# A two-layer decoder trunk on one core: a new table of weight slots, one modulation block moved to GpSimd, and more value groups between the output projections

## The chip, the core and the metric

The kernel runs on one core of a Trainium2 chip. TensorE (PE) multiplies and transposes, VectorE (DVE) does the elementwise work and the selections, ScalarE (ACT) copies out of PSUM and applies functions, GpSimd (POOL) computes a little and issues the gathers, and SyncE (SP) issues the weight loads. All transfers run on 16 DMA engines. The metric is the device time of one execution in microseconds; lower is better.

## What is computed

Two layers over 256 tokens of width 1024, all in float32, weights read from HBM. Cut from the reference:

```python
for l in range(DEPTH):                                   # DEPTH = 2
    mod = (silu(c) @ w_ada[l] + b_ada[l])                # six blocks of 1024
    sh1, sc1, g1, sh2, sc2, g2 = split(mod, 6)
    h = rms_norm(x) * (1.0 + sc1) + sh1
    q, k, v, qi, ki, wi, cu = split(h @ w_in[l], offs)
    attn = dsa_attention(q, k, v, qi, ki, wi)            # top-64 keys, causal
    conv = conformer_conv(cu, ...)                       # GLU, 31 causal taps, norm, silu
    mixed = concat([rms_norm(attn, ..), rms_norm(conv, ..)])
    x = x + g1 * (mixed @ w_out[l])
    h2 = rms_norm(x) * (1.0 + sc2) + sh2
    x = x + g2 * peer_ffn(h2, peer_wq[l], sub_keys[l], u[l], v[l])
```

`peer_ffn` picks 128 experts for every token (8 heads, 16 each). It gathers a row of `u` for each (4 KB), takes its dot product with `h2`, and sums the gathered rows of `v` with the resulting coefficients.

## The kernel before

**Parts.** A part `p` (0 to 3) is one layer `l = p // 2` with 128 tokens `t = p % 2`. For every part GpSimd issues 128 gathers of u rows and 128 of v rows, each 0.5 MB (128 tokens by 4 KB). They land in a ring of 13 row buffers, the tile `rows`. DVE takes one dot product per u row (L1512, function `dots_to`); PE sums four v rows in a group (L893, function `v_to`, 32 groups a part). While the rows of part p pass, PE, ACT and DVE compute projections, attention and expert choice of part p+1. Between GpSimd's gathers and their consumers there is only the ring: a buffer is used again when its dot (`u_used`) or its group (`v_used`) is done.

**Weights.** SP loads all weights in pieces of 1 MB, in the one order that `plan()` writes out. Every piece has a slot, and SP waits for the last user of the slot's former piece (`wait_weight_used`, loop at L609) before it issues the next. Nothing behind a waiting load is issued. Later on there are four slots (`wring`). In part 0, before the first gather, seven more exist. Slots 4 to 6 and 7, 8 lie in rows 6 to 11 and rows 0 to 3 of the row ring, slots 9 and 10 in `spread_c`. Rows 4 and 5 hold the convolution's accumulator `acc` and its temporaries `tap_tmp`. GpSimd's first gathers wait until the slot that shares their row buffer was used for the last time (`wait_slot_free`), and they are issued in order from row 0.

**Modulation blocks.** `mod` has twelve blocks of 4 MB each (four pieces). For most, PE multiplies the block (L760, 16 matmuls, job "ada") and turns the result later ("adaT"). DVE sums two of them, (0,2) and (0,4), with `ada_product`. The table `ADA` says where in each part a block is taken. Block (1,1), the scale of layer 2, is a PE product at place (0,"S"), in the middle of part 0's attention.

**Part 0, the path to the first gather.** DVE does 93 convolution tap steps for three of four channel groups, in pieces between its other work (`taps`, L1494). GpSimd does the fourth group by a TENSOR_SCALAR (L650) and a TENSOR_TENSOR (L651) for each tap. Then PE turns `acc`, DVE normalises (`conv_norm`, `join`, L1711), PE turns the mixed rows and projects them (L774), DVE adds to x and normalises, and PE projects the first expert queries (`wq` block 0, L802). DVE chooses 16 experts of head 0 and writes `u_at` (L1784), and the gathers begin. The blocks `wq` 1 to 3 (L788) follow on PE, with block (1,3) of the modulation between the second and the third.

**Later parts.** In `second(p)` PE mixes groups of the running v sum into the attention and the projections of the next part, by the table `V_GROUPS`. Then comes `mT` (two turns of the mixed rows), a wait for ACT's copy of them, and the four pieces of the output projection (L820), with a group behind the first three. On DVE, `qk_norms` (L1607 to L1612) runs without a break between runs of dots.

## Time and profile before

| | us |
|---|---|
| median of 3 runs | 1762.42 (1762.26 to 1763.1) |
| the profiled execution, device time | 1759.5 |
| its span, first to last instruction | 1757.2 |
| PE / DVE / POOL / ACT busy | 1020.7 / 1104.3 / 1021.9 / 262.9 |
| bytes moved | 693.84 MB at a mean of 395 GB/s |

A busy share near 60% on three engines says that none of them is full for long. The views to read are those of the DMA: its rate in each stretch of the span, and beside it which engine GpSimd's and SP's issues wait for. The table of 40 slices on the page shows a rate of 409 GB/s in the slices without a gap, and 249 GB/s in the lowest, around 150 us.

### The profile page before, as it was taken

Reading aid. Unit: us, or ns where it says so; the run is one execution under the profiler, and the core shown is the slowest. Engines: PE = TensorE matmul, PEld = TensorE weight load, DVE = VectorE, ACT = ScalarE, POOL = GpSimd, SP = SyncE. Lnnn points to the kernel's source line nnn. Section 1 sums busy time; section 2 is a strip of 40 time slices with the busy share of each in tenths; the row PEclk is TensorE's granted clock in tenths of the full one; section 3 lists DMA queues with packets and bytes.
Section 4 is the critical chain, followed back from the end, with each engine's and each line's share of the span. In section 5 each row is a group of like instructions: output and inputs, shape, how many; then the busy total and the mean of one; then the engine's idle time right before and its main releaser. Section 6 shows DMA issues by size and latency. Waiting matters only on the chain.

```text
span 1757.2 us, 17710 instructions
## 1 busy us (share of the span) xinstructions
PE 1020.7 (58%) x5918; PEld 566.7 (32%) x5918; DVE 1104.3 (63%) x3003; ACT 262.9 (15%) x710; POOL 1021.9 (58%) x1132
## 2 busy tenths in 40 slices
PE   5988796513887579611798568810679620004554
PEld 2646673311354156400246145600226300001111
DVE  1987997798218586889315766789622979991000
ACT  1131232301110024400100022600210100000000
POOL 2620535467654764566655674467655777776774
PEclk9978898556998779855799779965789965557888
DMA  9996999999999999999999999999999999999998
GB/s 351 389 346 249 405 402 409 409 380 409 393 409 401 409 409 395 396 410 410 406 368 408 409 406 404 409 409 409 404 385 408 400 411 410 409 410 404 409 409 325
DMA packets 199404, 693.84 MB, mean 395 GB/s; under 512 B 23943, under 2 KB 23959, under 8 KB 199315
## 3 DMA queue, kind: packets, MB, share of 16 engines
q0 software_dynamic: 147776, 537.19, 77.3%
...
HBM read 691.60 MB, written 1.05 MB: 394 GB/s over the span
## 4 chain that ended last, share of the span: by engine, by line
DMA 38%; PE 24%; DVE 15%; POOL 14%; issue 7%; ACT 1%; SPq 0%; POOLq 0%; DVEq 0%; ACTq 0%
DMA rows<-in_peer_v,v_at 18%; DMA rows<-in_peer_u,u_at 17%; PE ps L893 8%; DVE rows L1512 7%; POOL rows L667 7%; POOL rows L675 7%; PE ps L848 6%; DMA wring<-in_w_in 2%; PE ps L820 2%; DVE rows L1494 2%; PE ps L788 1%; DMA rows<-in_w_ada 1%; PE ps L836 1%; PE ps L706 1%; PE ps L774 1%
## 5 line engine op out<-in xcount | busy, mean ns | idle before, releaser
L667 POOL DMA_INDIRECT rows<-in_peer_u,u_at x512 | 482.8, 943 | 386.0 <-DVE dots L1512 213.1
L1512 DVE CUSTOM_DVE_ANT_0 rows<-rows,ps 128x1024 f32<-128x1024 f32 x512 | 609.8, 1219 | 101.5 <-DMA rows<-in_peer_u,u_at 88.7
L675 POOL DMA_INDIRECT rows<-in_peer_v,v_at x512 | 488.6, 954 | 281.4 <-PE ps L893 148.7
L893 PE MATMUL ps<-rows,spread_c 128*32 128x512 f32 x2048 | 324.8, 764 | 196.0 <-DMA rows<-in_peer_v,v_at 195.9
L706 PE MATMUL ps<-ident,coef 128*128 128x128 f32 x4 | 1.9, 475 | 349.7 <-DVE coef L1848 349.7
L893 PEld LDWEIGHTS ps<-rows,spread_c 128*32 128x32 f32 x2048 | 70.4, 126 | 399.1 <-issue 396.7
L848 PEld LDWEIGHTS ps<-hT,wring 128*128 128x128 f32 x1184 | 141.0, 200 | 25.3 <-issue 23.3
L848 PE MATMUL ps<-hT,wring 128*128 128x128 f32 x1184 | 146.3, 286 | 1.2 <-ACTq L1188 1.2
L820 PE MATMUL ps<-wring,hT 128*128 128x512 f32 x256 | 123.4, 627 | 13.3 <-DMA wring<-in_w_in 7.0
L1216 ACT ACTIVATE diag_eq<-ident,cwT 128x128 f32<-128x128 f32 x372 | 111.2, 387 | 31.6 <-PE ps L874 30.3
L706 PEld LDWEIGHTS ps<-ident,coef 128*128 128x128 f32 x4 | 0.7, 182 | 352.4 <-DVE coef L1848 352.4
L874 PE MATMUL ps<-diag_eq,hc 128*128 128x128 f32 x744 | 101.9, 301 | 19.9 <-ACT diag_eq L1216 19.9
L1525 DVE TENSOR_TENSOR gy<-ps,g 128x512 f32<-128x512 f32 x8 | 5.5, 690 | 163.2 <-PE ps L893 163.1
L874 PEld LDWEIGHTS ps<-diag_eq,hc 128*128 128x128 f32 x744 | 97.2, 213 | 27.1 <-ACT diag_eq L1216 25.3
L1716 DVE MAX8 v<-mixed_use 128x8 f32<-128x128 f32 x64 | 15.6, 285 | 121.0 <-ACTq L1176 119.1
L1173 ACT COPY mixed_use<-ps 128x512 f32<-128x512 f32 (+1 forms) x54 | 30.7, 569 | 300.9 <-PE ps L848 142.4
L820 PEld LDWEIGHTS ps<-wring,hT 128*128 128x128 f32 x256 | 48.4, 199 | 76.2 <-issue 57.3
L1815 DVE TENSOR_TENSOR gy<-ps,g 128x512 f32<-128x512 f32 x8 | 5.5, 692 | 81.2 <-PE ps L820 78.5
L1421 ACT ACTIVATE dots<-dots 128x128 f32<-128x128 f32 x4 | 1.2, 309 | 361.6 <-DVE dots L1512 361.6
L760 PE MATMUL ps<-wring,cact 128*32 128x512 f32 x208 | 32.1, 744 | 23.4 <-DMA wring<-in_w_ada 23.4
L1512 DVE DVE_READ_ACCUMULATOR2_ANT dots<- 128x1 f32 x512 | 42.2, 82 | 0.0
L1184 ACT ACTIVATE hT<-ps,modcol 128x128 f32<-128x128 f32 x52 | 19.5, 456 | 141.4 <-PE ps L706 140.6
...
## 6 DMA issues: line engine op xcount, KB each, us to landing
...
rows<-in_peer_u,u_at POOLq DMA_INDIRECT x512, 14.4
rows<-in_peer_v,v_at POOLq DMA_INDIRECT x512, 9.0
...
```

What stands on the lines that cost most here:

```text
L667: pool.indirect_dma_start(row(n), None, u_rows, bass.IndirectOffsetOnAxis(ap=u_at[:, p % 2, k:k + 1], axis=0)).then_inc(row_landed[n % SLO ...
L675: pool.indirect_dma_start(row(n), None, v_rows, bass.IndirectOffsetOnAxis(ap=v_at[:, p % 2, tok:tok + 1], axis=0)).then_inc(row_landed[n % ...
L706: ins = pe.transpose(o[:, i * n:(i + 1) * n], s, ident[0:n, 0:n])
L760: ins = pe.matmul(o[32 * g:32 * g + 32, :], cact[:, k:k + 1].to_broadcast([P, 32]), ws[:, i, 512 * cc:512 * cc + 512], start=h == 0, stop= ...
L820: ins = pe.matmul(o, lhs[:, k, :], w[:, j, 512 * cc:512 * cc + 512], start=k == 0, stop=k == KT - 1)
L848: ins = pe.matmul(o[:, i * P:(i + 1) * P], w[:, j, at:at + P], rhs[:, k, :], start=False, stop=(k, i) == (KT - 1, 3))
L874: ins = pe.matmul(o[:, cols], hc[:, ct, t * P + i:t * P + i + P], tap_diag(p, n, i - i0), start=False, stop=i == TAPS - 1)
L893: ins = pe.matmul(ps[32 * g:32 * g + 32, YB + q, :], spread_c[:, g, a, :], row(n)[:, q * 512:q * 512 + 512], start=a == 0, stop=a == 31)
L1173: act.copy(dst, o if src is None else src(o)).then_inc(free[b], 1)
L1216: ins = act.activation(tap_diag(p, n, i - i0), ident[:, :], ACT.Copy, scale=cwT[:, ct, i:i + 1])
L1494: seq_.lag(stt(o, hc[:, ct, i:i + P], w, o, ALU.mult, ALU.add))
L1512: dve.tensor_tensor_reduce(out=row(n), in0=row(n), in1=h2_shown, scale=1.0, scalar=0.0, op0=ALU.mult, op1=ALU.add, accum_out=dots[:, k:k + ...
```

## The change

- **A twelfth slot.** Rows 4 and 5 become slot 9 (`LATE_SLOT`), free once the convolution was turned (`conv_full`); the two slots in `spread_c` are now 10 and 11. The slots of part 0 from `sk` on come from a table (`SLOTS_OF`). All eight pieces of `wq` 0 to 3 have slots that don't wait for a `wq` before them, and the pieces of block (1,3) come behind them. The blocks that share row buffers 0 to 3 and 4 to 7 with gathers are now `wq` 1 and `wq` 2.
- **Block (1,1) goes to GpSimd.** It is neither in SP's order nor a PE product. GpSimd, behind its taps, loads it in four pieces through slots 7 and 8, and sums it with 8 TENSOR_SCALAR and 7 TENSOR_TENSOR of 128x1024 into half of `diag_eq`. SP waits for the end of that (`pool_ada_taken`) before it loads `wq` 1 into the same slots. PE turns the sum behind `wq` 3.
- **Block (1,3)** is multiplied behind `wq` 3, not between `wq` 1 and `wq` 2, and turned in the tail.
- **V groups.** One group of v rows is added between `mT` and the output projection in every part from 1 on; in parts 1 and 3 one more stands before the attention. Later groups move up by one.
- **Norms split.** `qk_norms` of parts 1 to 3 does 8 dots between the reciprocal roots and the multiplications. In part 1 the run of dots before it has 18, not 24.

```diff
-FIRST_WSLOTS = 11
+FIRST_WSLOTS = 12
+LATE_SLOT = 9
-V_GROUPS = [((4, 7), 8, (9, 10, 11), 12), ((4, 5, 6, 7), 9, (10, 11, 12), 13)]
+V_GROUPS = [(3, (4, 7), 8, 9, (10, 11, 12), 13), (4, (5, 6, 7, 8), 9, 10, (11, 12, 13), 14)]
+POOL_ADA = (1, 1)
+POOL_SLOTS = (7, 8)
-    (0, "S"): [product(1, 1), turn(1, 0), turn(1, 1)],
+    (0, "S"): [turn(1, 0)],
-    (0, "wq1"): [product(1, 3)],
-    (0, "wq2"): [turn(1, 3)],
-    (0, "tail"): [product(0, 5), product(1, 4), turn(0, 5), turn(1, 4)],
+    (0, "wq"): [turn(1, 1), product(1, 3)],
+    (0, "tail"): [turn(1, 3), product(0, 5), product(1, 4), turn(0, 5), turn(1, 4)],
+SLOTS_OF = {("sk", 0): (2,), ("ada", 0, 3): (3, 4, 5, 6), ("out", 0, 0): (0, 1), ("adav", 0, 4): (LATE_SLOT, 2, 3, 4),
+            ("out", 0, 1): (5, 6), ("wq", 0, 0): (0, 1), ("wq", 0, 1): POOL_SLOTS, ("wq", 0, 2): (LATE_SLOT, 4),
+            ("wq", 0, 3): (2, 3), ("ada", 1, 3): (0, 1, 2, 3)}
@@ SyncE
+                if name == ("wq", 0, 1):
+                    sp.wait_ge(pool_ada_taken, 4)
                 if use_before[i] is not None:
                     wait_weight_used(sp, use_before[i])
+                elif slot == LATE_SLOT:
+                    sp.wait_ge(conv_full, 1)
@@ GpSimd, behind the taps
+            for h in range(2):
+                wait_weight_used(pool, max(i for i, u in enumerate(uses) if slot_of[i] == POOL_SLOTS[h] and i < n_pool))
+                load_ada(h)
+            for h in range(4):
+                w = weight_slot(POOL_SLOTS[h % 2]).rearrange("p (k n) -> p k n", k=2)
+                pool.wait_ge(pool_ada_landed[h % 2], 16 * (h // 2 + 1))
+                for i in range(2):
+                    k = 2 * h + i
+                    dst = ada_sum if k == 0 else w[:, i, :]
+                    seq_(pool.tensor_scalar(dst, w[:, i, :], cact[:, k:k + 1], None, ALU.mult))
+                    if k:
+                        seq_(pool.tensor_tensor(ada_sum, ada_sum, w[:, i, :], ALU.add), pool_ada_taken if i else None)
+                if h < 2:
+                    load_ada(h + 2)
@@ TensorE, second(p)
                     v_to(p - 1, 2)
                     logits(p, CHUNKS[t][1])
-                    v_to(p - 1, 3)
-                    attend(p, at[0])
-                    v_to(p - 1, at[1])
+                    v_to(p - 1, at[0])
+                    attend(p, at[1])
+                    v_to(p - 1, at[2])
                 ... mT ...
+                v_to(p - 1, at[3])
                 pe.wait_ge(mixedT_ready, 2 * (p + 1))
@@ VectorE, qk_norms(p, between)
+                if between:
+                    between()
                 seq_(tt(qk, qk, rs[:, 0:16].unsqueeze(2).to_broadcast([P, 16, DH]), ALU.mult))
```

GpSimd's queue, from its last tap to its first gathers. Before:

```order
L650 TENSOR_SCALAR rows<-hc,cwT 128x128
L651 TENSOR_TENSOR rows<-rows 128x128
L667 DMA rows<-in_peer_u,u_at 128x1024 x96
L664 MEMSET spread_c 128x4096
L667 DMA rows<-in_peer_u,u_at 128x1024 x32
```

And now, up to the third of the block's four pieces:

```order
L666 TENSOR_SCALAR rows<-hc,cwT 128x128
L667 TENSOR_TENSOR rows<-rows 128x128
L674 DMA rows<-in_w_ada 128x2x1024 x2
L687 TENSOR_SCALAR diag_eq<-rows,cact 128x1024
L687 TENSOR_SCALAR rows<-rows,cact 128x1024
L689 TENSOR_TENSOR diag_eq<-diag_eq,rows 128x1024
L674 DMA rows<-in_w_ada 128x2x1024
L687 TENSOR_SCALAR rows<-rows,cact 128x1024
L689 TENSOR_TENSOR diag_eq<-diag_eq,rows 128x1024
L687 TENSOR_SCALAR rows<-rows,cact 128x1024
L689 TENSOR_TENSOR diag_eq<-diag_eq,rows 128x1024
L674 DMA rows<-in_w_ada 128x2x1024
```

Four loads and fifteen operations of 1024 columns now stand between the taps and the first gather.

SP's queue around `wq` (its weights are `in_peer_wq`), with what each load waits for. Before:

```order
L609 DMA rows<-in_peer_wq 128x4x512 [waits bank1_full]
L609 DMA rows<-in_peer_wq 128x4x512 [waits piece_used]
L609 DMA wring<-in_peer_wq 128x4x512 [waits ada_taken] x2
L609 DMA wring<-in_w_ada 128x2x1024 [waits ada_taken] x2
L609 DMA rows<-in_w_ada 128x2x1024 [waits piece_used]
L609 DMA rows<-in_w_ada 128x2x1024 [waits bank1_full]
L609 DMA wring<-in_peer_wq 128x4x512 [waits piece_used]
L609 DMA wring<-in_peer_wq 128x4x512 [waits bank2_full]
L609 DMA wring<-in_peer_wq 128x4x512 [waits piece_used] x2
```

And now, from the load that waits for the convolution:

```order
L625 DMA rows<-in_w_ada 128x2x1024 [waits conv_full]
L625 DMA wring<-in_w_ada 128x2x1024 [waits bank0_full]
L625 DMA wring<-in_w_ada 128x2x1024 [waits piece_used]
L625 DMA rows<-in_w_ada 128x2x1024 [waits piece_used]
L625 DMA rows<-in_w_out 128x4x512 [waits piece_used]
L625 DMA rows<-in_w_out 128x4x512 [waits bank3_full]
L625 DMA wring<-in_peer_wq 128x4x512 [waits piece_used]
L625 DMA wring<-in_peer_wq 128x4x512 [waits bank2_full]
L625 DMA rows<-in_peer_wq 128x4x512 [waits bank1_full,pool_ada_taken]
L625 DMA rows<-in_peer_wq 128x4x512 [waits piece_used,pool_ada_taken]
L625 DMA rows<-in_peer_wq 128x4x512 [waits ada_taken] x2
L625 DMA wring<-in_peer_wq 128x4x512 [waits ada_taken] x2
```

The last four pieces of `wq` wait for DVE's sum of block (0,4), where they waited for PE to be through with `wq` 1 and with block (1,3). One load waits for the convolution, and the next `wq` for GpSimd.

PE's queue in part 1, from the last values of the attention to the second piece of the output projection. Before, with L893 the groups of v rows:

```order
L918 MATMUL ps<-vals,mixed_use 128x64 x4
L893 MATMUL ps<-rows,spread_c 32x512 x16
L706 MATMUL ps<-ident,hb 128x128 x8
L820 MATMUL ps<-wring,hT 128x512 x4
L893 MATMUL ps<-rows,spread_c 32x512 x8
```

And now, with L935 the same groups:

```order
L960 MATMUL ps<-vals,mixed_use 128x64 x4
L935 MATMUL ps<-rows,spread_c 32x512 x8
L746 MATMUL ps<-ident,hb 128x128 x8
L935 MATMUL ps<-rows,spread_c 32x512 x8
L862 MATMUL ps<-wring,hT 128x512 x4
L935 MATMUL ps<-rows,spread_c 32x512 x8
```

One group stands between the turns of the mixed rows and the first piece of the projection.

## Rows read from the trace of the kernel before

**Rows 1.** The page: rates in 40 slices, and bytes of all transfers.
```profile
GB/s 351 389 346 249 405 402 409 409 380 409 393 409 401 409 409 395 396 410 410 406 368 408 409 406 404 409 409 409 404 385 408 400 411 410 409 410 404 409 409 325
DMA packets 199404, 693.84 MB, mean 395 GB/s; under 512 B 23943, under 2 KB 23959, under 8 KB 199315
```
**Rows 2.** Stretches: busy PE, PEld, DVE, ACT, POOL, then PEclk, DMA share, GB/s.
```profile
120.00:180.00 60.00, 52.27 (x304) 34.81 (x302) 42.01 (x148) 10.95 (x24) 4.89 (x5) 0.90 0.69 256
160.00:170.00 10.00, 10.00 (x92) 10.00 (x91) 6.42 (x38) 1.49 (x4) 0.00 (x0) 1.00 0.01 2
...
370.00:380.00 10.00, 1.11 (x4) 0.71 (x4) 9.86 (x19) 0.58 (x1) 5.54 (x6) 0.50 0.97 347
440.00:450.00 10.00, 10.00 (x83) 5.48 (x86) 6.01 (x16) 4.25 (x12) 7.56 (x9) 1.00 0.94 334
860.00:900.00 40.00, 32.65 (x144) 11.58 (x144) 10.65 (x33) 2.28 (x8) 23.03 (x24) 0.87 0.95 360
1280.00:1300.00 20.00, 17.90 (x73) 6.48 (x66) 0.00 (x0) 2.28 (x8) 10.60 (x12) 0.87 0.94 355
```
**Rows 3.** SP's timeline: start, length, merged loads.
```profile
105.19 21.55 SPq L609 DMA_DIRECT2D wring<-in_w_ada  x4
141.86 3.80 SPq L609 DMA_DIRECT2D rows<-in_w_ada  x2
171.80 5.02 SPq L609 DMA_DIRECT2D wring<-in_peer_wq  x4
```
**Rows 4.** DVE's timeline to the first experts: last taps, second norm of join, u_at.
```profile
105.57 6.13 DVE L1494 SCALAR_TENSOR_TENSOR rows<-hc,cwT,rows 128x128 f32<-128x128 f32 x23
114.24 0.70 DVE L1698 BATCH_NORM_STATS2 bn<-ps 128x6 f32<-128x512 f32 x1 [1.30 <-PE ps L1053]
125.89 0.48 DVE L1711 TENSOR_SCALAR hb<-hb,rs 128x512 f32<-128x512 f32 x1
172.62 0.17 DVE L1784 CAST u_at<-expert 128x16 uint32<-128x16 f32 x1
```
**Rows 5.** PE's timeline: turns of mixed rows, wq 1, wq 2.
```profile
128.82 1.09 PE L706 MATMUL ps<-ident,hb 128*128 128x128 f32 x8
165.35 7.31 PE L788 MATMUL ps<-hT,wring 128*128 128x128 f32 x64
181.83 9.01 PE L788 MATMUL ps<-hT,wring 128*128 128x128 f32 x64 [3.73 <-issue]
```
**Rows 6.** Single operations by line: shortest, median and longest in ns, and when.
```profile
L1494 DVE SCALAR_TENSOR_TENSOR rows<-hc,cwT,rows x2: 339/466/593, 98.3 to 98.6; 128x128 f32<-128x128 f32 x2
L1494 DVE SCALAR_TENSOR_TENSOR rows<-hc,cwT,rows x11: 339/341/343, 99.1 to 101.8; 128x128 f32<-128x128 f32 x11
L651 POOL TENSOR_TENSOR rows<-rows x30: 452/455/1101, 58.2 to 98.6; 128x128 f32<-128x128 f32 x30
L650 POOL TENSOR_SCALAR rows<-hc,cwT x30: 602/708/1662, 57.2 to 97.8; 128x128 f32<-128x128 f32 x30
L626 POOL TENSOR_TENSOR halves<-ident x1: 195/195/195, 2.9 to 2.9; 128x2 f32<-128x2 f32 x1
L664 POOL MEMSET spread_c<- x1: 3530/3530/3530, 355.5 to 355.5; 128x4096 f32 x1
```
**Rows 7.** POOL's timeline: last tap, first gather, a norm, v gathers.
```profile
98.60 0.45 POOL L651 TENSOR_TENSOR rows<-rows 128x128 f32<-128x128 f32 x1
173.67 1.10 POOL L667 DMA_INDIRECT rows<-in_peer_u,u_at  x1 [74.62 <-DVE u_at L1784]
725.20 0.94 POOL L667 DMA_INDIRECT rows<-in_peer_u,u_at  x1 [8.19 <-DVE dots L1512]
881.89 0.94 POOL L675 DMA_INDIRECT rows<-in_peer_v,v_at  x1 [8.00 <-PE ps L893]
```
**Rows 8.** PE's timeline in part 2, at the turns and the first projection piece.
```profile
869.92 1.09 PE L706 MATMUL ps<-ident,hb 128*128 128x128 f32 x8 [0.89 <-DVE hb L1711]
873.11 6.67 PE L820 MATMUL ps<-wring,hT 128*128 128x512 f32 x8 [2.10 <-ACTq L1188]
```

67 lines of the change are left out of this document (40 added, 27 removed).

## The prediction

> **What bounds the kernel now.** Read the page's line of rates first. In most of the 40 slices the core moves 405 to 411 GB/s, whatever the engines do, so the DMA is the full resource; the bytes are 693.84 MB [rows 1]. I take 409.5 GB/s as the full rate. All bytes at that rate are 1694.4 us, and the span is 1757.2 us, so the DMA has lost 62.8 us. The change moves no byte more or less. Its time is the old one plus what it changes in these losses.
>
> Next, where they lie. Between 120 and 180 us the rate is 256, a loss of 60 x (1 - 256/409.5) = 22.5 us, and from 160 to 170 nothing moves at all [rows 2]. The smaller holes, by the same formula: 860 to 900, 4.8 us; 1280 to 1300, 2.7; 440 to 450, 1.8; 370 to 380, 1.5 [rows 2]. Start, tail and slices slightly under the full rate make up the rest, and the change doesn't touch them.
>
> The large hole has two sides. SP has issued 54 pieces by 145.7 us and then nothing until 171.8 [rows 3]: every slot is held. The gathers start at 173.67, since POOL waited 74.62 us for `u_at` [rows 7]. So the end of the hole is set by the compute path to the first 16 experts. On that path, from about 99 us on, DVE is never idle for long: taps from 105.57, turned convolution at 114.24, second norm of `join` at 125.89 to 126.37, `u_at` at 172.62 [rows 4]. PE turns the mixed rows only at 128.82 [rows 5], 2.4 us after DVE was ready, since it was at block (0,3).
>
> **Part 1: the slots, with an unchanged path.** A piece is 1.05 MB, 2.56 us at full rate. Before, 54 pieces are in by about 158, and the next bytes flow at 173.5. Now the same 54 can be in (50 of SP, 4 of POOL), and two of block (1,3) follow when `wq` 0 is done, near 164 us: 56 pieces, 5.1 us more work before the gathers. But the gathers pay it back. Rows 0 to 3 share slots with `wq` 1, which PE ends at 172.7 [rows 5], so four gathers go. Row 4 shares its slot with `wq` 2. That block starts now at once, at about 174.5, since its weights are there and no product stands before it, and takes 7.3 to 9.0 us [rows 5]. Its first piece is free near 181.6. Four gathers are 2.1 MB or 5.1 us of work, in by about 180.7; the next bytes flow at about 183.4. That costs 2.7 us. Two small gaps come in besides: SP now stands at its late slot until the convolution is turned (about 114), and six pieces issued near 91 plus POOL's two last to about 112.5. Counting pieces up to the point where the DMA is full for good, before has moved 57.7 pieces by 183.5, and now 58 by 183.4. The slots alone are worth 1 us, no more: a gain in the hole that the row buffers give back. PE loses its product of (1,1), but it waits for DVE's taps behind it anyway, so that is worth nothing.
>
> **Part 2: POOL's sum, and what it does to DVE.** This is the largest term. In the last tap of POOL, a TENSOR_TENSOR from 98.60 to 99.05 [rows 7], DVE's tap of 98.6 took 593 ns; the eleven taps after it, with POOL idle, took 341 [rows 6]. A DVE operation with two SBUF inputs stands still while POOL's two-input operation runs, for 0.25 us of its 0.452. In the other direction, POOL's shortest TENSOR_TENSOR is 452 ns and its longest 1101 [rows 6], beside a DVE operation of 1024 columns. POOL's TENSOR_TENSOR grows from 195 ns at 2 columns to 452 at 128 [rows 6], 2.04 ns a column; at 1024 it is 2.28 us, and holds DVE for about 2.28 - 0.2 = 2.1. There are seven: 14.7 us. POOL's TENSOR_SCALAR takes 602 ns at 128 columns [rows 6]. For 1024 the lower bound is 602 plus 896 columns at the memset's 0.86 ns (3530/4096, rows 6), 1.37 us, and the upper 8 x 602, 4.8 us. I take 1.4: the 195 ns row shows that most of a short operation is fixed cost. Next to it the DVE taps show no delay that I can see, at 128 columns.
>
> When does it happen? POOL's two first loads are issued at 99.5 and share the DMA with SP's, so they land near 107 and 112. A column block costs 1.4 + 2.3 + 0.2 us, so the eight and their loads run from 107 to about 138. In that stretch DVE is on the path. Laying seven holds of 2.1 us over DVE's own row of operations moves the end of `join` from 126.3 to about 138.5; 12.1 us arrive there, since two fall partly on waits. The 2.4 us that DVE was early go off. So the mixed rows are turned 9.7 us later, and with them `u_at`, the first gather and the end of the hole: **plus 9.7 us**, minus the 1 us of part 1. The DMA can't use that time: SP has no free slot. `pool_ada_taken` at 138 costs nothing: SP comes to that wait at 138.4 plus 9.7, and `wq` 1 is needed at 165.4 plus 9.7. At the upper price of TENSOR_SCALAR POOL ends near 161; `wq` 1 then lands by 169, still in time, and queued behind it are `wq` 2 and 3 only.
>
> The Trainium skill says more (SBUF — State Buffer, "Who interferes with whom"): the pair of ports is an exclusive lock for the whole instruction, and a DVE operation with two SBUF inputs contends with any GpSimd operation that reads SBUF. The rows on TENSOR_TENSOR agree. By that rule TENSOR_SCALAR of 1024 columns holds DVE too, which no row here shows; it is the slower rival below.
>
> **Part 3: v groups.** In part 2, PE ends the turns at 871.0 and idles 2.10 us for ACT's copy, then a projection piece takes 6.67 us, and POOL waits 8.00 us until 881.89 for a group [rows 7, 8]. A group is 1.92 us of PE work and fits into that idle time; its rows have landed, since groups arrive every 5.1 us and the last began at 865.4. POOL gets four buffers at about 872.9 and doesn't stop at all, and in-flight rows cover the 6.67 us. Of the 4.8 us I take 4.5. The hole at 1280 to 1300 is the same figure in part 3: 2.4 of 2.7. At 440 the group before the attention frees four buffers some 6 us sooner: 1.6 of 1.8. Sum 8.5 us. Low end 4, if PE has to wait for the added group's rows and brings the projection later; high end 9.3, all of it.
>
> **Part 4: split norms.** POOL stops 8.19 us at 717 to 725 for DVE's norms [rows 7], as it does in part 1 at 368. With 8 dots in the middle (8 x 1.28 us, the pace of the DMA) both stops are shorter than what is in flight. I count the 1.5 us of 370 to 380 [rows 2] less 0.3, and 0.9 for the smaller ones in parts 2 and 3: 2.0 us, between 0.5 and 3. Its price is that `qk_ready` comes 10 us later, hidden behind PE's wait for the coefficients.
>
> **Sum.** +9.7 - 1 - 8.5 - 2.0 = -1.8 us. From the profiled execution's 1759.5 that is 1757.7; the median lies 2.9 us above the profiled one, so 1762.42 - 1.8 = 1760.6.
>
> **Rivals.** (a) *The holds don't grow with the operation.* 128 columns can't tell a lock of a whole instruction from one of short chunks. If POOL lets DVE in between chunks, DVE loses perhaps 0.25 us for each of 7, or a third of the 14.7: the path moves 0 to 6 us. For it speaks that the taps beside TENSOR_SCALAR don't suffer; against it that DVE's blocked tap ended only when POOL's did. Time: 1762.4 - 1 - 10.5 + (0 to 6), 1751 to 1757. (b) *POOL's TENSOR_SCALAR holds DVE too*, for the 0.88 us in which 1024 columns stream at the memset's rate. Eight of them are 7 us, of which DVE gives way to about half between its own operations: the path moves by 13.3, not 9.7, and the v groups and norms can't outweigh it if they bring 8 or less. Sum 13.3 - 1 - 8 = +4.3: 1766.7, slower. It decides from a delay of `u_at` by more than 15 us on, or from 13 with a poor part 3. If TENSOR_SCALAR costs its upper 4.8 us and holds as well, the delay passes 20 and the time 1770. (c) *The groups bring little*, since PE waits for rows as it does with most groups now: part 3 is 4 and the sum +2.7: 1765. (d) *The GpSimd sum is hidden after all*, as its loads land later than I think and the holds fall on DVE's waits behind 126: that gives the times of (a).
>
> **How the numbers follow.** Forecast (delay 8 to 12 us): 0.40. Rival (a) and (d): 0.32. Rival (b): 0.18. Rival (c): 0.10. The forecast's own range is 1757 to 1765. A measurement of this kernel tells 0.2% or 3.5 us from no change. Faster by more than that: all of (a) and (d), and 0.08 of the forecast: 0.40. Slower: 0.14 of (b) and 0.05 of (c): 0.19. The rest, 0.41, is within. The range that leaves 2 in 10 out goes from 1752.5 to 1768.
>
> **What would show it.** In the trace after: the first gather near 183 us, not 173.7; DVE taps between 107 and 116 with single durations over 2 us, each ending with a TENSOR_TENSOR of POOL (2.3 us); POOL's TENSOR_SCALAR near 1.4 us; a second gap in the DMA after the fourth gather, 2 to 3 us long; 860 to 900 and 1280 to 1300 at 400 GB/s or more; POOL's waits of 8 us at 717 and 874 gone. If the first gather stays near 174, the forecast is too high by 9 us. If `wq` 1 keeps PE waiting for its weights, POOL's sum took longer than its upper price, and part 2 is wrong there.

## The result, and the profile after

The changed kernel takes 1770.84 us (median of 7 runs, 1769.77 to 1772.79). The kernel before, run beside it, takes 1762.42 us (median of 7, 1760.82 to 1766.78). The ratio is 1.0045, 95% interval 1.0034 to 1.0055: slower by 8 us. The forecast was 1760.6, and its range ended at 1768.0. The profiled execution took 1770.62 us, with a span of 1768.8.

The page again first, the rates in 40 slices and the bytes, as in [rows 1]:

```profile
GB/s 354 381 297 276 304 402 409 409 389 395 409 409 402 409 408 400 403 402 409 398 409 405 401 396 405 409 409 409 394 384 409 409 410 410 409 410 405 409 409 326
DMA packets 199403, 693.84 MB, mean 392 GB/s; under 512 B 23942, under 2 KB 23958, under 8 KB 199314
```

The bytes are the same and the full slices are as full as before. The third to fifth slice are worse together (297, 276, 304 for 346, 249, 405). The same stretches as in [rows 2], moved where the later start moves them (busy PE, PEld, DVE, ACT, POOL, then PEclk, DMA share, GB/s):

```profile
120.00:180.00 60.00, 46.77 (x216) 30.66 (x216) 47.70 (x87) 10.20 (x23) 36.45 (x15) 0.76 0.77 272
140.00:160.00 20.00, 19.63 (x59) 10.32 (x59) 19.46 (x13) 0.17 (x1) 17.58 (x6) 0.84 0.50 152
180.00:190.00 10.00, 9.28 (x83) 9.09 (x82) 8.97 (x49) 1.17 (x2) 2.06 (x3) 1.00 0.47 170
380.00:420.00 40.00, 7.81 (x24) 5.62 (x24) 39.55 (x71) 4.24 (x6) 26.61 (x29) 0.50 0.98 371
440.00:450.00 10.00, 6.60 (x41) 1.95 (x38) 8.27 (x24) 1.09 (x4) 7.57 (x9) 0.83 1.03 409
860.00:900.00 40.00, 32.03 (x176) 11.04 (x169) 5.99 (x23) 4.79 (x11) 29.54 (x33) 0.88 1.02 409
1300.00:1320.00 20.00, 20.00 (x90) 6.40 (x81) 0.00 (x0) 0.62 (x3) 11.81 (x13) 0.93 0.96 352
```

The hole before the first gather is now two holes, 140 to 160 and 180 to 190. The holes at 440 and at 860 to 900 are gone. Those at 380 to 420 (before 370 to 390) and at 1300 to 1320 (before 1280 to 1300) stay. With the formula of the prediction in stretches of 10 us, the losses up to 240 us are 47.4 us, before 33.8. From 240 to 1620 us, in stretches of 20, they are 18.0, before 19.8. So the whole increase lies ahead of 240 us.

There the first gather has moved by 13.7 us from the 173.67 of [rows 7]. GpSimd's timeline in the changed kernel, for its sum and the first gathers:

```profile
109.95 5.32 POOL L687 TENSOR_SCALAR diag_eq<-rows,cact 128x1024 f32<-128x1024 f32 x1 [8.20 <-DMA rows<-in_w_ada]
115.36 2.84 POOL L687 TENSOR_SCALAR rows<-rows,cact 128x1024 f32<-128x1024 f32 x1
118.29 2.37 POOL L689 TENSOR_TENSOR diag_eq<-diag_eq,rows 128x1024 f32<-128x1024 f32 x1
...
155.23 2.79 POOL L689 TENSOR_TENSOR diag_eq<-diag_eq,rows 128x1024 f32<-128x1024 f32 x1
187.33 1.08 POOL L707 DMA_INDIRECT rows<-in_peer_u,u_at  x1 [29.31 <-DVE u_at L1828]
...
194.73 1.11 POOL L707 DMA_INDIRECT rows<-in_peer_u,u_at  x1 [2.58 <-PE ps L830]
```

A TENSOR_SCALAR of 1024 columns takes 2.84 us undisturbed, not 1.4; the first took 5.32, beside DVE's taps. A TENSOR_TENSOR takes 2.37 to 2.79. The sum therefore ends at 158.0 us, not at 138. The fifth gather waits 2.58 us for `wq` 2: that is the second gap of part 1, forecast at 2.7.

DVE's timeline in the same kernel, for the taps beside the first TENSOR_SCALAR, operations of the convolution's norm and of the second norm of `join`, two steps of DVE's own sum of block (0,4), and the operation that reads PE's second output block:

```profile
106.43 6.13 DVE L1536 SCALAR_TENSOR_TENSOR rows<-hc,cwT,rows 128x128 f32<-128x128 f32 x23
...
119.28 1.92 DVE L1746 TENSOR_TENSOR hb<-hb,ln_gb 128x512 f32<-128x512 f32 x1
121.24 2.19 DVE L1747 TENSOR_TENSOR hb<-hb,ln_gb 128x512 f32<-128x512 f32 x1
...
125.35 2.00 DVE L1480 SCALAR_TENSOR_TENSOR newt<-rs,halfv 128x1 f32<-128x1 f32 x1
...
129.24 1.32 DVE L1755 TENSOR_SCALAR hb<-hb,rs 128x512 f32<-128x512 f32 x1
130.59 2.71 DVE L1492 CUSTOM_DVE_ANT_0 gy<-hb 128x512 f32<-128x512 f32 x1
...
142.52 3.25 DVE L1524 SCALAR_TENSOR_TENSOR rows<-wring,cact,rows 128x1024 f32<-128x1024 f32 x1
145.80 2.02 DVE L1525 SCALAR_TENSOR_TENSOR rows<-wring,cact,rows 128x1024 f32<-128x1024 f32 x1
...
158.60 0.69 DVE L1859 TENSOR_TENSOR gy<-ps,g 128x512 f32<-128x512 f32 x1
```

The 23 taps take 6.13 us, exactly as in [rows 4], although GpSimd's TENSOR_SCALAR runs beside the last 2.6 of them. The forecast had single taps of over 2 us there; there are none. After 118.29, when the first TENSOR_TENSOR begins, operations take 1.92 and 2.19 us instead of 0.69, a step of one column 2.00 instead of 0.22, and the root's sum of squares 2.71 instead of 0.69. Not all of these lie beside a TENSOR_TENSOR: the 2.19 us at 121.24 begin after the first one has ended (120.66), while GpSimd issues a load (120.95 to 121.71) and starts its next TENSOR_SCALAR (121.76). In the sum of (0,4) steps take 3.25 and 2.02 us instead of 1.28. PE's timeline shows what this passes on:

```profile
137.05 1.97 PE L746 MATMUL ps<-ident,hb 128*128 128x128 f32 x8 [7.10 <-DVE hb L1755]
140.37 9.79 PE L816 MATMUL ps<-wring,hT 128*128 128x512 f32 x16 [1.35 <-DVEq L1852]
149.99 7.03 PE L816 MATMUL ps<-rows,hT 128*128 128x512 f32 x16
...
179.01 7.31 PE L830 MATMUL ps<-hT,rows 128*128 128x128 f32 x64
```

The mixed rows are turned at 137.05, 8.2 us later than in [rows 5], after an idle time of 7.10 us. The first block of the output projection then takes 9.79 us; in the kernel before, the same 16 matmuls are the first half of the 14.00 us that the two blocks take together. The granted clock is 0.60 from 130 to 140 and 0.71 from 140 to 150. The second block ends at 157.02, and DVE reads it at 158.60 without having waited for it; in the kernel before, DVE waited 2.62 us for that block. So the path runs through DVE's sum here and not through PE's slower block. `wq` 1 begins at 179.01, against 165.35.

The result and the first set of runs (`e1_no_sum` to `e4_slots_pe`) fell on times at which the kernel before took 1762 to 1764 us. The later sets, those of every label that ends in `_only` but `e2_scale_only`, in `_mended`, `_again` or `_third`, fell on times at which the kernel before itself took 1946 to 1949 us. Its trace then has waits of PE, ACT and DVE under "issue" and "remote" in all parts (of ACT up to 54.8 us at a time), where the first trace has none of ACT and DVE and none of PE over 5.5 us; that the engines waited for their own instructions is my reading of these names and is not shown. The ratios of these sets are compared with one another and not with those of the first set.

### The profile page after: what moved, and what is told of

It reads as the page before. It is cut to its first block, busy times and chain, and to the rows that moved or that the text cites. A ratio compares the mean times of both kernels' runs of the same rounds, so it can differ in the third digit from the quotient of the medians.

```text
span 1768.8 us, 17681 instructions
## 1 busy us (share of the span) xinstructions
PE 1023.6 (58%) x5894; PEld 569.9 (32%) x5894; DVE 1120.9 (63%) x3003; ACT 263.0 (15%) x709; POOL 1071.1 (61%) x1151
## 4 chain that ended last, share of the span: by engine, by line
DMA 40%; DVE 21%; PE 19%; POOL 13%; issue 6%; ACT 1%; SPq 0%; DVEq 0%; POOLq 0%; ACTq 0%
DMA rows<-in_peer_v,v_at 19%; DMA rows<-in_peer_u,u_at 17%; DVE rows L1554 9%; PE ps L935 7%; POOL rows L715 7%; PE ps L890 6%; POOL rows L707 6%; DMA wring<-in_w_in 2%; DMA rows<-in_w_ada 1%; PE ps L862 1%; PE ps L878 1%; DVE rows L1536 1%; PE ps L816 1%; DVE newt L1480 1%; PE ps L746 1%
## 5 line engine op out<-in xcount | busy, mean ns | idle before, releaser
L935 PE MATMUL ps<-rows,spread_c 128*32 128x512 f32 x2048 | 329.1, 773 | 206.1 <-DMA rows<-in_peer_v,v_at 206.0
L935 PEld LDWEIGHTS ps<-rows,spread_c 128*32 128x32 f32 x2048 | 71.3, 127 | 405.4 <-issue 403.1
L862 PE MATMUL ps<-wring,hT 128*128 128x512 f32 x256 | 117.1, 600 | 8.2 <-DMA wring<-in_w_in 7.7
L746 PE MATMUL ps<-ident,hb 128*128 128x128 f32 x88 | 19.4, 394 | 37.0 <-DVE hb L1616 16.3
```

Source lines behind the costliest of these rows:

```text
L746: ins = pe.transpose(o[:, i * n:(i + 1) * n], s, ident[0:n, 0:n])
L862: ins = pe.matmul(o, lhs[:, k, :], w[:, j, 512 * cc:512 * cc + 512], start=k == 0, stop=k == KT - 1)
L935: ins = pe.matmul(ps[32 * g:32 * g + 32, YB + q, :], spread_c[:, g, a, :], row(n)[:, q * 512:q * 512 + 512], start=a == 0, stop=a == 31)
```

## Experiments

**Which part of GpSimd's block moves the path?** Three kernels take the changed one and leave out operations of the sum; the loads, the slots and all waits stay.

```diff
@@ e1_no_sum: no arithmetic
-                    seq_(pool.tensor_scalar(dst, w[:, i, :], cact[:, k:k + 1], None, ALU.mult))
-                    if k:
-                        seq_(pool.tensor_tensor(ada_sum, ada_sum, w[:, i, :], ALU.add), ...)
+                    if k == 0:
+                        seq_(pool.memset(ada_sum, 0.0))
@@ e2_scale_only: the 8 TENSOR_SCALAR stay
-                    if k:
-                        seq_(pool.tensor_tensor(ada_sum, ada_sum, w[:, i, :], ALU.add), ...)
@@ e6_add_only: the 7 TENSOR_TENSOR stay
-                    seq_(pool.tensor_scalar(dst, w[:, i, :], cact[:, k:k + 1], None, ALU.mult))
```

> The kernel after, with GpSimd's loads of block (1,1) kept and its 15 operations of 1024 columns left out (a MEMSET of zeros stands for the sum, so the scale of layer 2 lacks this block). Theory H: GpSimd's TENSOR_TENSOR holds DVE, and that alone moves the path to u_at. Then DVE's join ends near 127 us again, the mixed rows are turned near 129, out(0,0) takes about 7 us and not 9.8, the first gather stands within 2 us of 173.7 (after: 187.3), and the time is 1770.8 - 13.7 = about 1757, 1756 to 1760. Rival S (the new slots, the wait of SP at its late slot, the sharing of the DMA with GpSimd's loads): the first gather stays later than 180 and the time above 1765.

Measured: 1758.94 us beside 1763.53 of the kernel before, ratio 0.9977 (0.9963 to 0.9991). The first gather, the turns of the mixed rows and the first output block of this kernel, from GpSimd's and PE's timelines:

```profile
172.60 1.06 POOL L707 DMA_INDIRECT rows<-in_peer_u,u_at  x1 [58.97 <-DVE u_at L1828]
...
128.37 1.10 PE L746 MATMUL ps<-ident,hb 128*128 128x128 f32 x8
130.81 7.13 PE L816 MATMUL ps<-wring,hT 128*128 128x512 f32 x16 [1.35 <-DVEq L1852]
```

All three are back where they were, and the output block takes 7.13 us. Against the ratio 1.0045 of the full change the arithmetic costs 0.0068 of 1763 us, 12.0 us. The rival that blamed slots, SP's wait at the late slot, or the sharing of the DMA falls: all of these are in this kernel. What it doesn't have is SP's late release by `pool_ada_taken`; the kernel with the additions alone, below, ends its sum at 133 us and still has the late first gather, so that wait isn't what moves the path.

> The kernel after with GpSimd's 8 TENSOR_SCALAR of 1024 columns kept and its 7 TENSOR_TENSOR left out (the products are made, their sum is not). Theory H (only the TENSOR_TENSOR holds DVE): the first gather is within 1.5 us of that of the kernel without any arithmetic, so 174 to 176, and the time within 2 us of that kernel's. Rival L (a lock by any GpSimd instruction with an SBUF input, as my rival b had it): the first gather is 4 to 7 us later than without arithmetic, 179 to 182, and the time 4 to 7 us above. DVE's operations beside a TENSOR_SCALAR: no single one over 1 us by H, several at 2 us or more by L.

Measured: 1759.28 us, ratio 0.9981 (0.9967 to 0.9995), 0.3 us above the kernel without arithmetic. By time alone, theory H holds. The traces say otherwise of its reason. Three operations of DVE in the norms, and GpSimd's last TENSOR_SCALARs, in the kernel with scaling alone:

```profile
119.33 1.69 DVE L1745 TENSOR_TENSOR hb<-hb,ln_gb 128x512 f32<-128x512 f32 x1
...
126.04 1.85 DVE L1491 CUSTOM_DVE_ANT_0 gy<-hb 128x512 f32<-128x512 f32 x1
...
129.28 1.01 DVE L1483 SCALAR_TENSOR_TENSOR rs<-newt,rs 128x1 f32<-128x1 f32 x1
...
119.34 5.79 POOL L687 TENSOR_SCALAR rows<-rows,cact 128x1024 f32<-128x1024 f32 x2
...
126.22 11.91 POOL L687 TENSOR_SCALAR rows<-rows,cact 128x1024 f32<-128x1024 f32 x4
```

DVE's TENSOR_TENSOR takes 1.69 us, 1.00 more than its usual 0.69, and it began with GpSimd's TENSOR_SCALAR at 119.34. The two others are 1.16 and 0.85 us over theirs; they too begin within 0.2 us of a TENSOR_SCALAR. So a TENSOR_SCALAR does hold DVE's operations with two SBUF inputs, for about 1 us at its start and not for its 2.9; what DVE does in the rest of it takes its usual time in this trace. In the changed kernel one row doesn't fit: DVE's TENSOR_SCALAR at 129.24 takes 1.32 us instead of 0.49, though GpSimd's TENSOR_SCALAR had begun at 127.44, and ends (130.56) just after that one does (130.29). Why that happens there and not here (the same line takes 0.49 us at 130.33) is open. The last operation of `join` begins 14.5 us after the convolution's statistics here (115.80 to 130.33), and 11.7 without arithmetic. But PE, which came to the mixed rows 2.4 us late in any case, swallows nearly all of these 2.9 us. My expectation had "no single one over 1 us" for H: that is wrong, and rival L is right about the mechanism and wrong about the time.

> The kernel after with GpSimd's 7 TENSOR_TENSOR kept and its 8 TENSOR_SCALAR left out (a MEMSET starts the sum; the block isn't scaled by silu(c)). Times from the first statistics of the convolution to the first gather: after 71.6 us, scaling only 59.4, neither 58.7. If only TENSOR_TENSOR holds DVE, all the 12.8 us stay: 71 to 72 and a time of 1770. If both hold, and the 2.4 us that DVE is early cover the first of it, it is 58.7 + (7 x 2.0, less what falls after the path or on waits, less 2.4), about 67 to 70, and the time 1766 to 1769.

The times of this kernel are from the later conditions (1915.39 us beside 1945.94, ratio 0.9846, 0.9803 to 0.9890) and say nothing on the path. Its trace up to the first gather does. DVE's last step of the taps, GpSimd's second and third TENSOR_TENSOR, and the first gather:

```profile
111.35 5.65 DVE L1539 SCALAR_TENSOR_TENSOR rows<-hc,cwT,rows 128x128 f32<-128x128 f32 x3
...
114.49 4.78 POOL L687 TENSOR_TENSOR diag_eq<-diag_eq,rows 128x1024 f32<-128x1024 f32 x2
...
184.07 1.06 POOL L707 DMA_INDIRECT rows<-in_peer_u,u_at  x1 [50.98 <-DVE u_at L1828]
```

Three taps of together 1.12 us take 5.65: they end with the first of these two TENSOR_TENSOR, and the one before (109.52 to 113.45) held them as well. From statistics to first gather it is 65.8 us, below the 67 to 70 expected, since here one of the holds falls before the statistics. The last tap of GpSimd is the better mark, since nothing of the change lies before it and executions differ by up to 3 us there (98.15 to 101.17 in these traces). From it to the first gather, in one execution of each:

| kernel | last tap | first gather | between |
|---|---|---|---|
| before | 98.60 | 173.67 | 75.1 |
| e1_no_sum | 98.23 | 172.60 | 74.4 |
| e2_scale_only | 99.51 | 175.20 | 75.7 |
| e6_add_only | 98.15 | 184.07 | 85.9 |
| after | 99.46 | 187.33 | 87.9 |
| e4_slots_pe | 101.17 | 178.19 | 77.0 |

Adding alone costs 11.5 us, scaling alone 1.3, both 13.5. On top of adding, scaling costs 2.0. The figure for adding is the weakest, since it comes from the later conditions: the twelve traces without the sum there spread from 74 to 78 us (`before_again` 74.8, `n_third` 78.0).

In this kernel DVE isn't held in its sum of (0,4), and there PE's slower block is on the path: it takes 8.85 us instead of 7.13, and DVE waits 4.34 us for the second block instead of 2.62.

**Is the rest of the change worth having?** Two kernels separate it from the sum. The first is the kernel before with the new v groups and split norms. The second keeps the whole change, but gives block (1,1) back to SP and PE, and SP's wait for GpSimd goes:

```diff
@@ e4_slots_pe, from the changed kernel
-    (0, "S"): [turn(1, 0)],
+    (0, "S"): [product(1, 1), turn(1, 0), turn(1, 1)],
-    (0, "wq"): [turn(1, 1), product(1, 3)],
+    (0, "wq"): [product(1, 3)],
+SLOTS_OF = {("ada", 1, 1): (7, 8, 0, 1), ("sk", 0): (2,), ("ada", 0, 3): (3, 4, 5, 6), ("out", 0, 0): (7, 8),
+            ("adav", 0, 4): (0, 1, LATE_SLOT, 2), ("out", 0, 1): (3, 4), ("wq", 0, 0): (5, 6), ("wq", 0, 1): (7, 8),
+            ("wq", 0, 3): (0, 1), ("wq", 0, 2): (LATE_SLOT, 4), ("ada", 1, 3): (2, 3, 0, 1)}
```

> The kernel before with only the changed v groups and the split norms. My prediction had 8.5 + 2.0 = 10.5 us for these two: 1752. From the trace of the kernel after (DMA losses from 240 us to 1620 us 17.3 against 20.1 before) it would be 2.8: 1759.6. The hole at 1280 to 1300 stays if it belongs to the groups themselves, and is gone if it came from the later start of everything in the kernel after.

> The kernel after with block (1,1) back on SP and PE: loaded behind (0,2)'s place as before, multiplied by PE in the middle of part 0's attention. Late slot, table of slots, wq behind one another, v groups and norms stay as in the kernel after. By theory H the first gather comes back to 174 to 176 and the time is 1762.4 - 2.8 - 1 = 1758 to 1760, so it is faster than both kernels. By rival S (slots and order of loads cost the time) the first gather is later than 180 and the time above 1765.

Measured: 1757.77 us, ratio 0.9966 (0.9954 to 0.9978), and 1757.87 us, ratio 0.9964 (0.9951 to 0.9977). Both beat both kernels. Groups and norms together bring 6.0 us (3.9 to 8.1), between the 10.5 of the prediction and the 2.8 that the trace of the changed kernel alone suggested. That trace misled me, since the profiled execution of the kernel before was itself 3 to 4 us better than its median; I had noted the 2.9 us in the prediction and then compared two traces without it. The kernel before scatters from 1757.1 to 1769.6 over 34 runs, this one from 1755.4 to 1760.0 over 12.

The slots bring nothing measurable: with them it is 0.9964, without 0.9966. The first gather of `e4_slots_pe` is at 178.19, later than the 174 to 176 expected. The gap behind the fourth gather is there as in the changed kernel. GpSimd's timeline, fifth gather:

```profile
185.58 1.10 POOL L680 DMA_INDIRECT rows<-in_peer_u,u_at  x1 [2.54 <-PE ps L801]
```

The path is also 2.6 us longer than in `e1_no_sum` (table). DVE is ready for the mixed rows at 128.89 and PE turns them at 132.69, while in `e1_no_sum` it is 125.99 and 128.37: PE, with a product more ahead of it, is 1.4 us of that later. Up to 240 us this kernel loses 38.1 us of DMA time, and `e3_groups_norms` 35.4 with its first gather 2.8 us sooner (175.36): the trace shows no gain from the slots to set against the later gather.

**Why do two holes stay?** In the kernel with groups and norms, the windows that held the holes, DVE's and GpSimd's timelines in the norms of part 1, and PE's timeline at the mixed rows of part 3:

```profile
1280.00:1300.00 20.00, 15.51 (x68) 5.67 (x68) 4.33 (x17) 2.28 (x8) 12.21 (x14) 0.83 0.96 360
360.00:400.00 40.00, 7.81 (x24) 5.61 (x24) 39.17 (x76) 4.23 (x6) 24.98 (x27) 0.50 0.98 368
860.00:900.00 40.00, 30.23 (x149) 10.50 (x144) 8.93 (x27) 2.28 (x8) 26.67 (x29) 0.95 1.03 409
...
358.98 1.81 DVE L1610 TENSOR_SCALAR halfv<-halfv 128x16 f32<-128x16 f32 x1
...
357.22 3.53 POOL L664 MEMSET spread_c<- 128x4096 f32 x1
...
1284.91 1.97 PE L706 MATMUL ps<-ident,hb 128*128 128x128 f32 x8 [4.50 <-DVE hb L1714]
```

The hole at 860 to 900 is full here (409, before 360). At 1280 to 1300 it is 360, before 355, and PE waits 4.50 us for DVE's mixed rows. My theory was that the group of v rows added ahead of the attention delays everything behind it. The other kernels of the first set have the same table of groups, and their traces can be laid beside it: from PE's turn of the coefficients to its turn of the mixed rows, in us, and the slowest stretches of 20 us between 420 and 1340, in GB/s.

| kernel | part 1 | part 2 | part 3 | slowest 20 us |
|---|---|---|---|---|
| before | 45.5 | 43.6 | 47.6 | 880 to 900, 340; 1280 to 1300, 355 |
| after | 46.9 | 43.3 | 50.5 | 1300 to 1320, 352 |
| e3_groups_norms | 45.7 | 43.6 | 50.5 | 1280 to 1300, 360; 1240 to 1260, 362 |
| e1_no_sum | 47.7 | 43.5 | 48.9 | 460 to 480, 377 |
| e2_scale_only | 45.9 | 45.9 | 48.6 | 880 to 900, 352 |
| e4_slots_pe | 46.5 | 45.3 | 48.6 | 880 to 900, 352 |

With one table the hole falls in part 3 in two kernels, in part 2 in two, and in part 1 in one. Each time PE has waited 4.5 to 5.0 us for DVE's mixed rows and turns them in 1.97 us instead of 1.09, at the lower clock (granted 0.68 from 1280 to 1290 in `e3_groups_norms`). Part 2 has no group added ahead of its attention. So the added group alone doesn't put the hole at 1280 to 1300: where there is no hole it makes part 3 about 1 us longer than before (48.6 to 48.9 beside 47.6), and where the rest falls is open. Nor is the hole at 860 to 900 gone for good: with the same groups it is 378 and 381 GB/s in `e2_scale_only` and `e4_slots_pe`.

In the norms, a TENSOR_SCALAR of 16 columns takes 1.81 us instead of 0.17, and ends at 360.79, when GpSimd's MEMSET of 3.53 us ends. The split starts the norms 6 dots sooner, and that is beside the MEMSET. The Trainium skill (SBUF — State Buffer, "Who interferes with whom") says that `tensor_scalar` is among DVE's operations that can enter a mode which takes the port pair shared with GpSimd, and that in this mode DVE contends with GpSimd; this row agrees. The same section calls the pair an exclusive lock, held for a whole instruction: of TENSOR_TENSOR the traces here agree (DVE's step of one column at 125.35 ends at 127.35, GpSimd's TENSOR_TENSOR at 127.34), of TENSOR_SCALAR beside DVE's operations with two SBUF inputs they don't (1.0 us of 2.9).

Kernels with the groups alone and with the norms alone, and one that takes the added group of part 3 away and moves the MEMSET, were then run:

```diff
@@ e5_mended and mended_*, from e3_groups_norms
-                at = V_GROUPS[t]
+                at = V_GROUPS[t] if p != 3 else (3, (4, 5, 6, 7), 9, 10, (11, 12, 13), 14)
-                    if (p, k) == (0, 96):
+                    if (p, k) == (0, 112):
```

`v_only`, `v_again` and `v_third` are the kernel before with the first of the two edits of the change (`V_GROUPS` and the `v_to` calls), `n_only`, `n_again` and `n_third` with the second (`qk_norms`). `e7_slots_pe_mended` and `e7_third` are `e4_slots_pe` with the two lines above.

> The kernel before with the changed v groups alone. With both, groups and norms, the time was 0.9966 of before, -6.0 us (-4 to -8). If my shares of 8.5 for the groups and 2.0 for the norms are right in proportion, the groups alone bring -4.8 us. From that kernel's trace I expect more of it here than that: the hole at 860 to 900 (4.8 us) and the one at 440 (1.7) are gone, the one at 1280 to 1300 (2.4) stays, since the group added before the attention of part 3 delays the mixed rows. So -6.5 plus what comes back elsewhere: 0.9965, 0.995 to 0.998.

> The kernel before with the split norms alone. My prediction had -2.0 us. From the trace of groups and norms together: in part 1 the losses at 360 to 400 are 4.1 us against 3.2 before, at 720 they are less by 1.4 and at 740 more by 1.0. So it brings nothing: 0.999 to 1.001. In part 1 DVE's TENSOR_SCALAR of 16 columns inside the norms (0.17 us) takes 1.8 us again, ending with GpSimd's MEMSET, if that MEMSET is what held it.

> Before with groups and norms, and two things mended. In part 3 the group added before the attention is taken away: groups 3, (4 to 7), 9, 10 stand where 4, (5 to 8), 9, 10 stood. And GpSimd's MEMSET of the spread matrix stands before gather 112 of part 0, not before gather 96. If the hole at 1280 to 1300 comes from the delayed attention, the mixed rows are turned near 1279 and not 1285, GpSimd's wait of 3.6 us is gone, and 2 to 4 us are won. If the MEMSET held DVE's norms, the losses at 360 to 400 fall from 4.1 by 1 to 1.6 us. Together 1757.8 - 3 to 5: 1753 to 1755, ratio 0.9945. If the theory of the added group is wrong, the ratio stays at 0.996 to 0.997.

All of them fell on the later conditions, and so did every repetition:

> The kernel before with the changed v groups alone, a second time, since the runs of v_only fell on a chip on which the kernel before takes 1946 us and PE waits for its own instructions. Same expectation on a chip of 1763 us: the holes at 860 to 900 and at 440 gone, the one at 1280 to 1300 kept, 0.9965, 0.995 to 0.998. If the groups bring what the prediction's share says, -4.8 us or 0.9973.

> The kernel before with the split norms alone, a second time, for the same reason. Prediction -2.0 us (0.9989); from the trace of groups and norms together nothing: 0.999 to 1.001. On the other chip the TENSOR_SCALAR of 16 columns inside the norms took 3.08 us; here it should again end with GpSimd's MEMSET of 3.5 us.

> Before with groups and norms and the two things mended (no added group before the attention of part 3; the MEMSET before gather 112). The mixed rows of part 3 are turned near 1279, not 1285, no wait of GpSimd over 3 us near 1290, the TENSOR_SCALAR of 16 columns takes 0.17 us, losses at 360 to 400 down by 1 to 1.6 us. Together 3 to 5 us less than groups and norms as they were (1757.8): 1753 to 1755, ratio 0.9945. If the theory of the added group is wrong, 0.996 to 0.997.

> The kernel with the new table of slots, block (1,1) on PE and SP, groups and norms, and the same two things mended. The slots were worth nothing (1757.9 beside 1757.8 for groups and norms alone), since what they gain in the hole the gap behind the fourth gather takes back. So this stays within 1.5 us of the mended kernel without the slots: 1753 to 1756. If it is below 1752, the slots do gain where part 1 of the prediction said 1 us.

> The kernel before with the changed v groups alone; v_only and v_again fell into calls in which every kernel took 9% to 10% longer and all engines waited for their own instructions. In a call in which the kernel before takes 1763 us: the holes at 860 to 900 and at 440 gone, the one at 1280 to 1300 kept, 0.9965, 0.995 to 0.998. By the prediction's share -4.8 us or 0.9973, by its full figure -8.5 us or 0.9952.

> The kernel before with the split norms alone. Prediction -2.0 us (0.9989); from the trace of groups and norms together nothing, 0.999 to 1.001. In the two calls with slow instructions it was 0.986 and 0.984; if that was theirs and not the kernel's, it is gone here. If the norms do bring 1.4% everywhere, it stays.

> Before with groups and norms and the two things mended (no added group before the attention of part 3; the MEMSET before gather 112, where it held no operation of the norms in the two calls before). The mixed rows of part 3 are turned near 1279, not 1285, no wait of GpSimd over 3 us near 1290. 3 to 5 us less than groups and norms as they were (0.9966): 0.9940 to 0.9950. If the theory of the added group is wrong, 0.996 to 0.997.

> New table of slots, block (1,1) on PE and SP, groups and norms, and both mended. The slots were worth nothing, so it stays within 1.5 us of the mended kernel without them: 0.993 to 0.996. Below 0.9925 the slots do gain where part 1 of the prediction said 1 us.

| kernel | ratios to the kernel before, at 1946 to 1949 us | intervals |
|---|---|---|
| v groups alone | 0.9938, 0.9963, 0.9938 | 0.9908 to 0.9990 |
| split norms alone | 0.9860, 0.9844, 0.9857 | 0.9802 to 0.9902 |
| both, mended | 0.9815, 0.9830, 0.9815 | 0.9770 to 0.9869 |
| both, mended, with slots and PE's block (1,1) | 0.9786, 0.9781 | 0.9736 to 0.9826 |

None of the sizes expected can be read from these. The kernels with slots stand 0.0044 and 0.0034 below those without, with intervals that overlap, so a gain from the slots isn't excluded there. The local steps can be read. At the mixed rows of part 3, PE's timeline with the v groups alone and with the mended table, the turn of the coefficients and that of the mixed rows:

```profile
1369.43 0.47 PE L706 MATMUL ps<-ident,coef 128*128 128x128 f32 x1 [0.84 <-DVE coef L1849]
...
1424.36 0.90 PE L706 MATMUL ps<-ident,hb 128*128 128x128 f32 x3 [3.53 <-DVE hb L1712]
...
1352.16 0.47 PE L706 MATMUL ps<-ident,coef 128*128 128x128 f32 x1 [10.53 <-DVE coef L1851]
...
1400.24 1.09 PE L706 MATMUL ps<-ident,hb 128*128 128x128 f32 x8 [2.69 <-issue]
```

It is 54.9 us with the added group, 48.1 without, and 49.5 in the kernel before under the same conditions (1368.32 to 1417.81). Over all these traces it is 54.9 to 55.7 in the three with v groups alone, 48.1 to 52.8 in the five without the added group in part 3 (`mended` and `e7`), and 51.1 to 53.1 in the three with the old groups and the norms split. So under these conditions the added group does delay the mixed rows, by some us, as the theory says. It does so in part 1 as well (53.7 to 55.5 us with it, 48.8 to 49.3 without). That it is worth 2 to 4 us of the whole time was not shown. For the MEMSET, single operations by line in the norms of part 1, with the split norms alone and with the MEMSET moved (mean in ns behind the busy time):

```profile
L1609 DVE TENSOR_SCALAR halfv<-halfv 128x16 f32<-128x16 f32 x1 | 3.1, 3083 | 0.0
...
L1610 DVE TENSOR_SCALAR halfv<-halfv 128x16 f32<-128x16 f32 x1 | 0.2, 174 | 0.0
```

3083 ns beside the MEMSET, 174 without (1064 ns in the changed kernel itself, in the result's trace). Here too the mechanism is shown and its worth, at most 1.6 us on the conditions of the result, is not.

**Where do 1.4% for the norms come from?** The prediction's part 4 had 0.1%, and the first trace nothing. The last two labels are the kernel before, for its trace under those conditions (one execution, 1935.83 us, beside a median of 1946.77), and the changed kernel.

> The kernel before itself, for its trace. If the conditions are those of the last three calls, it takes about 1948 us, with waits of PE and ACT for instructions, and its losses against the kernel with split norms (1917) show where that one wins there: in the stretches around the norms by the theory that the norms matter, spread over all parts if it is only a matter of which waits hide the slow instructions. If the conditions are those of the first call, it takes 1763 us and shows the scatter of one execution against another up to the end of the convolution (114.2 us in the first trace).

> The kernel after itself. Under the conditions of the result its ratio is 1.0045. If instructions are slow again: the path to the first gather is longer by the same 13 us (first gather near 190), and the rest gains what the kernels with groups, norms and the sum gained there (0.985), so 0.984 to 0.990. If the sum costs the same everywhere and the gains too, 1.0045.

The changed kernel takes 1916.96 us beside 1946.77, ratio 0.9846 (0.9815 to 0.9876). Its first gather is at 187.93, 13.2 us further from GpSimd's last tap than in `before_again` (88.0 and 74.8 us). So the sum delays the first gather by the same 13 us, and the verdict turns round all the same. What DVE waits for at the coefficients, from the waits of the kernel before, of that with v groups alone, with norms alone, and of the changed one (us in total, times, longest):

```profile
DVE coef L1848 <- ACT dots L1421: 66.5, 3, 24.3
...
DVE coef L1849 <- ACT dots L1422: 69.8, 4, 23.6
...
DVE coef L1850 <- ACT dots L1421: 29.8, 2, 18.7
...
DVE coef L1892 <- ACT dots L1463: 31.8, 2, 18.6
```

DVE waits 66.5 and 69.8 us for ACT where the norms are in one piece, 29.8 and 31.8 where they are split. In the first trace of the kernel before this wait is 1.5 us. Under the later conditions ACT comes late to the activation between the dots and the coefficients, up to 24.3 us at a time, and PE's first group and GpSimd's v gathers stand behind that. For the norms alone that is 36.7 us less wait; between the two executions traced the time is 22.8 us shorter (1935.83 and 1913.08), and by the three ratios 27 to 30. The two go together; that the one makes the other is not shown. A second, smaller gain is the one that the split is made for. GpSimd's wait at the norms of part 2, in the kernel before and with the norms split:

```profile
791.25 0.94 POOL L667 DMA_INDIRECT rows<-in_peer_u,u_at  x1 [27.63 <-DVE dots L1512]
...
789.09 0.94 POOL L667 DMA_INDIRECT rows<-in_peer_u,u_at  x1 [21.95 <-DVE dots L1512]
```

27.63 us become 21.95: DVE comes 20 us late to the norms, and then every microsecond to the first dot counts. Why ACT comes later to the coefficients where the norms are whole, I did not find; it may be no more than which of ACT's waits under "remote" falls on that place.

## Why the prediction was wrong

**What bounds the kernel** was right: full slices unchanged, bytes unchanged, and the whole change of time in the holes.

**Part 1, the slots: -1 forecast, 0 found.** The second gap is there with the size forecast (2.58 us), and the hole's gain is given back. `e4_slots_pe` against `e3_groups_norms` is 0.0002 of the time. The two small gaps that the forecast had in the fill are larger: 110 to 130 us run at 191 and 249 GB/s, before at 393 and 199, which is 3.7 us more of loss; that this took the last microsecond is argued, not shown.

**Part 2, GpSimd's sum: +9.7 forecast, 13.7 in the trace and 12.0 by the runs.** Of the 13.7 us, 0.9 lie ahead of GpSimd's last tap (99.46, before 98.60), so the trace gives the sum 12.8. This is the step that failed. That a TENSOR_TENSOR holds DVE was right: six of the seven met an operation of DVE and held it for 1.2 to 2.0 us, where I had seven of 2.1. These terms were wrong:
- The price of TENSOR_SCALAR was taken as 1.4 us from the MEMSET's pace, "the 195 ns row shows that most of a short operation is fixed cost". It is 2.84. The bounds given, 1.37 and 4.8, held it.
- The hold by TENSOR_SCALAR was put at nothing, on taps beside 128 columns. Up to the end of `join`, at 137.0, DVE's operations in the changed kernel take 10.4 us more than their usual times. 5.0 of them lie beside three TENSOR_TENSORs, 4.2 beside TENSOR_SCALARs or the load issues just ahead of them, and 1.2 in two of DVE's own TENSOR_SCALARs.
- What was counted too high: the holds before 137. From GpSimd's last tap to the end of `join` it is 37.5 us, and 27.8 in `e1_no_sum`: 9.8 us, where I laid 12.1. That the two are so near is partly luck: I had all the holds of TENSOR_TENSOR in there and none of TENSOR_SCALAR.
- The sum lasted to 158 and not to 138. I laid seven holds over the rows up to 138 and stopped. Those at 142 to 157 fall on the sum of (0,4) and on the addition to x: from the mixed rows' turn (8.2 us late) to that of `h2` (163.66, 13.2 us late) another 5 us are lost. DVE is held for 6.7 us there, and 2.6 of that is the wait for PE's second block that it no longer has: 4.1 us. The other 0.9 is PE's turn of the mixed rows, 1.97 us instead of 1.09, at the lower clock behind 7.10 us of idle time.
- The sum had no term for what a longer wait does to PE. On the path of the changed kernel that is the 0.9 us and another 0.4 in `wq` 0 (8.38 us, before 7.94). The 2.7 us that the first output block takes longer cost nothing here, since DVE comes later still; had DVE not been held in that stretch, PE's blocks would have set its end about 1.5 us sooner, at 157.0.

Rival (b) is near to what happened: TENSOR_SCALAR holds DVE too, for about 1 us where it said 0.88, and the delay came out at 13.7 (12.8 behind the last tap) where it said 13.3. Its time of 1766.7 is 4.1 too low, since it still took 8 us for groups and norms and 1 for the slots. The runs put the scaling at 1.3 us alone and 2.0 on top of the adding; alone it is mostly covered by the 2.4 us that PE comes late in any case. I gave (b) 0.18, on the taps beside 128 columns, which showed no delay; beside 1024 columns the taps showed none either, since taps in close order keep GpSimd out (5.32 us for its operation) instead of being held. Only the three taps behind the first short pause, at 112.66, took 1.80 us instead of 1.12.

`pool_ada_taken` was said to cost nothing. SP's timeline has `wq` 1 issued at 158.05, when the sum ends, though the two pieces before it were out by 150.55; it landed in time for PE at 179.01, as the prediction's upper price said. The DMA runs at 152 GB/s from 140 to 160, but at the end of the hole every slot is full again, so this wait cost nothing that the trace shows; no run takes it away by itself.

**Parts 3 and 4: -10.5 forecast, -6.0 found.** In the changed kernel the 4.8 us of 860 to 900 and the 1.8 at 440 came as forecast, and the 2.4 at 1280 to 1300 did not. The step "is the same figure in part 3" is the one that failed: it counted every hole as filled, while each of the five traces with these groups keeps one of 1.6 to 2.8 us, in part 1, 2 or 3. Part 3 also gets a group ahead of the attention, which was counted as a gain at 440 only. The norms' 1.5 us at 370 to 380 did not come: losses from 360 to 400 are 4.1 us with the split (380 to 420 in the changed kernel, 3.8), 3.2 before. DVE's stop after the second run of dots took the first one's place, and 1.6 us went to the MEMSET. How much of the 6.0 belongs to each was not settled on those conditions.

**Sum.** 12.0 + 0 - 6.0 = +6 from the experiments, +8 measured, within their intervals of about 2 us each. The forecast was -1.8, and all terms erred to the same side: GpSimd's sum by 2.3 us by the runs (3.1 by the trace), groups and norms by 4.5, the slots by 1.
